# Softmax weights turned by VectorE and ScalarE, and the head norm behind the next pair's softmax

## The reference

```python
scores = einsum('bqhmd,bkhmd->bhmqk', q_blk, k) * scale      # m: the two halves of a head
scores = where(causal, scores, NEG_BIG)
probs = softmax(scores, axis=-1)
weights = probs[:, :, 0] - lam * probs[:, :, 1]
o = einsum('bhqk,bkhe->bqhe', weights, v)                    # then: RMS norm of o over the head,
branch = concatenate([o_normed, cross_out]) * silu(gate)     # and the gate
y = branch @ w_out[i]
```

## Time and profile before

| | |
|---|---|
| median of 3 runs | 956.64 us (955.88 to 961.71) |
| the profiled execution, its own time | 955.9 us |
| its span, first to last instruction | 954.1 us |
| TensorE busy | 943.2 us (99%), granted clock 0.997 |
| VectorE busy | 630.6 us (66%) |
| ScalarE busy | 474.9 us (50%) |

### The profile page before, as it was taken

How to read it: one execution, slowest core, us unless ns; L and a number is a source line. 1 busy time by engine, 2 the same in 40 slices (tenths; PEclk the granted TensorE clock), 3 DMA queues, 4 the chain that set the end, 5 groups by cost and what they waited for, 6 DMA issues and landing times.

```text
span 954.1 us, 14081 instructions
## 1 busy us (share of the span) xinstructions
PE 943.2 (99%) x5148; PEld 810.9 (85%) x5148; DVE 630.6 (66%) x868; ACT 474.9 (50%) x726; POOL 1.2 (0%) x9
## 2 busy tenths in 40 slices
PE   8999999999999999999999999999999999999996
PEld 7888888888888888888888888888888888888885
DVE  5877665666666666655595546457878778886555
ACT  6767544444444443344465355345465465464541
POOL 0000000000000000000000000000000000000000
PEclk9999999999999999999999999999999999999998
DMA  9757466666666665665576646565655755746562
GB/s 337 235 168 261 153 186 197 200 191 190 191 185 194 184 191 189 208 192 190 181 230 191 196 133 208 168 201 167 202 175 160 219 167 165 218 136 212 188 192 91
DMA packets 148778, 182.31 MB, mean 191 GB/s; under 512 B 8128, under 2 KB 116992, under 8 KB 147968
## 3 DMA queue, kind: packets, MB, share of 16 engines
q1 hardware_dynamic: 147792, 177.25, 59.8%
q10 hardware_dynamic: 944, 4.49, 1.2%
HBM read 176.48 MB, written 2.10 MB: 187 GB/s over the span
## 4 chain that ended last, share of the span: by engine, by line
PE 98%; DVE 1%; DMA 0%; ACT 0%; issue 0%; DVEq 0%; SPq 0%; ACTq 0%
PE psum L370 40%; PE psum L371 20%; PE psum L431 10%; PE psum L433 10%; PE psum L432 10%; PE psum L382 1%; PE psum L450 1%; PE psum L607 1%; PE psum L475 1%; PE psum L458 1%; PE psum L383 1%; DMA raw_ring<-in_w_kv_mem_dram 0%; PE psum L579 0%; PE psum L467 0%; PE psum L590 0%; PE psum L589 0%
## 5 line engine op out<-in xcount | busy, mean ns | idle before, releaser
L370 PE MATMUL psum<-hT_split,hi_ring 128*128 128x512 f32 x1600 | 559.3, 395 | 0.0
L923 DVE TENSOR_TENSOR lo_ring<-raw_ring,hi_ring 128x1024 fp32r<-128x1024 f32 x318 | 384.9, 1223 | 247.0 <-ACT hi_ring L656 245.5
L656 ACT ACTIVATE hi_ring<-raw_ring 128x1024 fp32r<-128x1024 f32 x318 | 335.3, 1062 | 392.8 <-PE psum L371 257.4
L371 PE MATMUL psum<-hT_split,lo_ring 128*128 128x256 f32 x1600 | 444.2, 278 | 0.0
L370 PEld LDWEIGHTS psum<-hT_split,hi_ring 128*128 128x128 f32 x1600 | 300.0, 188 | 70.5 <-issue 2.0
L371 PEld LDWEIGHTS psum<-hT_split,lo_ring 128*128 128x128 f32 x1600 | 300.7, 188 | 0.1
L431 PE MATMUL psum<-hi_ring,branchT_split 128*128 128x512 f32 x256 | 99.9, 390 | 0.0
L433 PE MATMUL psum<-hi_ring,branchT_split 128*128 128x512 f32 x256 | 99.6, 389 | 0.0
L432 PE MATMUL psum<-lo_ring,branchT_split 128*128 128x512 f32 x256 | 99.6, 389 | 0.0
L433 PEld LDWEIGHTS psum<-hi_ring,branchT_split 128*128 128x128 f32 x256 | 48.0, 188 | 10.0
L431 PEld LDWEIGHTS psum<-hi_ring,branchT_split 128*128 128x128 f32 x256 | 48.1, 188 | 10.0
(11 more groups left out here) (185 smaller groups left out, 675.7 us busy)
## 6 DMA issues: line engine op xcount, KB each, us to landing
raw_ring<-in_w_in_dram SPq DMA_DIRECT2D x224, 512.0 KB, 4.5
raw_ring<-in_w_out_dram SPq DMA_DIRECT2D x64, 512.0 KB, 4.8
raw_ring<-in_w_kv_mem_dram SPq DMA_DIRECT2D x30, 512.0 KB, 4.8
layer_area<-layer_area SPq DMA_DIRECT2D x48, 64.0 KB, 3.2
...
```

The source lines that it names most:

```text
L370: mm(o, hi[:, k, P * c:P * (c + 1)], X[:, kt, :], start=kt == 0, stop=False)
L371: last = mm(o[:, SEQ:], lo[:, k, P * c:P * (c + 1)], X[:, kt, 0:SEQ], start=False, stop=kt == KT - 1)
L656: run(whi[:, slot, :], raw[:, slot, :], ACT.Copy).then_inc(hi_ready, 1)
L923: V_.tensor_tensor(wlo[:, slot, :], raw[:, slot, :], whi[:, slot, :].bitcast(f32), SUB)\
```

## The change

`diff_turn` is gone from TensorE. VectorE turns the weights as 32x32 blocks in one instruction behind `softmax_weights` (`V_.transpose`, into the half of `prob` that is no longer needed). ScalarE then moves the blocks to their places: 16 copies of 32 partitions by 192 elements (`move_weights`), eight ahead of the key group's unit 1 and eight ahead of unit 2, in place of the one copy out of PSUM. The values (`diff_values`, `take_values`) move from key group 3 to gate group 1. `out_norm` of pair p-2 moves to VectorE's query group 3, behind the weights of pair p-1; `diff_out_turn` of p-2 to key group 3; `out_take` of p-2 to gate group 1. So the output side runs one pair later. Two sets of `o_eps` keep the sums of two pairs apart.

At the end, the output side of pair 4 and all of pair 5 behind its weights slide into the first output group. The order in which this group takes its units is changed (`OUT1_ORDER`), with the columns of pair 4 and 5 last. VectorE's loop over pairs now covers pairs 2 to 5, where it covered 1 to 4.

```diff
@@ -28,7 +28,8 @@
 XGATE_COL = GATE_COL + TOK_WIDTH
-OUT_ORDER = [0, 2, 4, 6, 8, 12, 14, 10]
+OUT0_ORDER = [0, 2, 4, 6, 8, 12, 14, 10]
+OUT1_ORDER = [0, 2, 4, 6, 12, 14, 8, 10]
 STORES = [(0, 0, 1024), (0, 1024, 2048)] + [(1, ACOLS * g, ACOLS * (g + 1)) for g in range(4)]
...
@@ -135,6 +136,8 @@
     probT = L1[:, 4608:5376].rearrange("p (h k) -> p h k", h=2)
+    prob_blocks = prob[:, :, 1, :]
+    QUADRANTS = [(a, b) for a in range(4) for b in range(4)]
     o_sb = l1(5376).rearrange("p (g e) -> p g e", g=4)
...
@@ -321,7 +324,7 @@
         for g in range(4):
-            row_group(U_OUT1 + A_UNITS * g, w_out[1], ACOLS * g, OUT_ORDER)
+            row_group(U_OUT1 + A_UNITS * g, w_out[1], ACOLS * g, OUT1_ORDER)
         for n, (t, lo_col, hi_col) in enumerate(STORES):
...
@@ -571,17 +574,8 @@
                 cross_values(1)
-        def diff_turn(p):
-
-            pe.wait_ge(w_ready, p + 1)
-            for h in range(2):
-                for b in range(3):
-                    last = nc.tensor.transpose(ps[:, 4 + h, P * b:P * (b + 1)],
-                                               prob[:, h, 0, P * b:P * (b + 1)], ident)
-            last.then_inc(wt_done, 1)
-
         def diff_values(p):
-            pe.wait_ge(wt_ready, p + 1)
+            pe.wait_ge(wt_ready, p * 16 + 16)
             for h in range(2):
...
@@ -590,8 +584,10 @@
             last.then_inc(pv_done, 1)
-        def diff_out_turn(p):
+        def diff_out_turn(p, exps=None):
             pe.wait_ge(on_ready, p + 1)
+            if exps is not None:
+                pe.wait_ge(exp_done, exps)
             for g in range(4):
...
@@ -610,10 +606,15 @@
             G, u = p * 3 + G_PAIR, p * (3 * B_UNITS) + U_PAIR
-            column_group(G, u, s, XA, at={} if first else {1: lambda: diff_scores(p - 1, second)})
-            column_group(G + 1, u + B_UNITS, 1 - s, XA,
-                         at={} if first else {2: lambda: diff_turn(p - 1), 3: lambda: diff_values(p - 1)})
-            column_group(G + 2, u + 2 * B_UNITS, s, XA, at={} if first else {2: lambda: diff_out_turn(p - 1)})
+            in_query, in_keys, in_gate = {}, {}, {}
+            if not first:
+                in_query[1] = lambda: diff_scores(p - 1, second)
+                in_gate[1] = lambda: diff_values(p - 1)
+            if not first and not second:
+                in_keys[3] = lambda: diff_out_turn(p - 2, p * 8)
+            column_group(G, u, s, XA, at=in_query)
+            column_group(G + 1, u + B_UNITS, 1 - s, XA, at=in_keys)
+            column_group(G + 2, u + 2 * B_UNITS, s, XA, at=in_gate)
         pair(0, G_PAIR % 2, first=True)
...
@@ -621,17 +622,18 @@
             pair(p + 1, (G_PAIR + 1) % 2)
-        column_group(G_XG1, U_XG1, G_XG1 % 2, XA, at={1: lambda: diff_scores(PAIRS - 1)})
+        column_group(G_XG1, U_XG1, G_XG1 % 2, XA,
+                     at={1: lambda: diff_scores(PAIRS - 1)})
         column_group(G_XG1 + 1, U_XG1 + B_UNITS, (G_XG1 + 1) % 2, XA,
-                     at={2: lambda: diff_turn(PAIRS - 1), 3: lambda: diff_values(PAIRS - 1)})
+                     at={3: lambda: diff_out_turn(PAIRS - 2, PAIRS * 8)})
         done0 = PAIRS + 1
...
                 y_wait(4 + g - 2)
-            row_group(G_OUT1 + g, U_OUT1 + A_UNITS * g, (G_OUT1 + g) % 2, XC, OUT_ORDER,
-                      before=branch_wait({0: done0 + PAIRS - 1, 5: done0 + PAIRS, 6: done0 + PAIRS + 1,
-                                          7: done0 + PAIRS + 2}),
-                      at={4: lambda: diff_out_turn(PAIRS - 1)} if g == 0 else {},
+            row_group(G_OUT1 + g, U_OUT1 + A_UNITS * g, (G_OUT1 + g) % 2, XC, OUT1_ORDER,
+                      before=branch_wait({0: done0 + PAIRS - 2, 4: done0 + PAIRS - 1, 5: done0 + PAIRS,
+                                          6: done0 + PAIRS + 1, 7: done0 + PAIRS + 2}),
+                      at={1: lambda: diff_values(PAIRS - 1), 5: lambda: diff_out_turn(PAIRS - 1)} if g == 0 else {},
                       half_first=g == 3)
...
@@ -867,9 +869,12 @@
                 cross_take(1)
-        def take_weights(p):
-            act.wait_ge(wt_done, p + 1)
-            run(probT, ps[:, 4:6, 0:3 * P], ACT.Copy).then_inc(wt_ready, 1)
+        def move_weights(p, first, last):
+            act.wait_ge(blocks_turned, p + 1)
+            for a, b in QUADRANTS[first:last]:
+                to = probT.rearrange("p h (k a r) -> p h k a r", k=3, a=4)[32 * b:32 * b + 32, :, :, a, :]
+                block = prob_blocks.rearrange("p h (k b r) -> p h k b r", k=3, b=4)[32 * a:32 * a + 32, :, :, b, :]
+                run(to, block, ACT.Copy).then_inc(wt_ready, 1)
         def take_values(p):
...
@@ -892,8 +897,8 @@
             column_group(G + 1, u + B_UNITS, 1 - s,
-                         at={} if first else {2: lambda: take_weights(p - 1), 3: lambda: take_values(p - 1)})
-            column_group(G + 2, u + 2 * B_UNITS, s)
+                         at={} if first else {1: lambda: move_weights(p - 1, 0, 8), 2: lambda: move_weights(p - 1, 8, 16)})
+            column_group(G + 2, u + 2 * B_UNITS, s, at={} if first else {1: lambda: take_values(p - 1)})
             tanh_of(G + 2, val1, tanh1)
...
@@ -904,10 +909,11 @@
         column_group(G_XG1 + 1, U_XG1 + B_UNITS, (G_XG1 + 1) % 2,
-                     at={2: lambda: take_weights(PAIRS - 1), 3: lambda: take_values(PAIRS - 1)})
+                     at={1: lambda: move_weights(PAIRS - 1, 0, 8), 2: lambda: move_weights(PAIRS - 1, 8, 16)})
         tanh_of(G_XG1 + 1, val1, tanh1)
         for g in range(4):
-            out_group(4 + g, U_OUT1 + A_UNITS * g, (G_OUT1 + g) % 2, at={1: begin_roots} if g == 1 else {})
+            out_group(4 + g, U_OUT1 + A_UNITS * g, (G_OUT1 + g) % 2,
+                      at={1: begin_roots} if g == 1 else {1: lambda: take_values(PAIRS - 1)} if g == 0 else {})
     @block.vector
...
@@ -1238,6 +1244,7 @@
         V_.tensor_copy(crossT1, cross_o).then_inc(xo_taken, 1)
+        V_.memset(cols[:, 100:101], 0.0).then_inc(o_taken, 1)
         cos2 = cosT.unsqueeze(1).broadcast_to([P, 2, SEQ])
...
@@ -1255,10 +1262,10 @@
             V_.tensor_tensor(t, t, rot, ADD).then_inc(rope_done, 1)
-        def out_norm(st, p):
+        def out_norm(st, p, parity):
             dve.wait_ge(o_copied, p * 5 + 5)
-            rsqrt(st, o_rstd, ss[:, 4:8], HEAD_DIM, o_eps)
+            rsqrt(st, o_rstd, ss[:, 4:8], HEAD_DIM, o_eps[parity])
             st.need()
...
@@ -1297,8 +1304,10 @@
             last.then_inc(w_ready, 1)
-
-        def pair(st, p, s, parity, first=False):
+            dve.wait_ge(w_ready, p + 1)
+            V_.transpose(prob_blocks, prob[:, :, 0, :]).then_inc(blocks_turned, 1)
+
+        def pair(st, p, s, parity, first=False, second=False):
             G, c, u = p * 3 + G_PAIR, p * 3 + columns_before(G_PAIR, 9), p * (3 * B_UNITS) + U_PAIR
...
@@ -1306,27 +1315,28 @@
                 rope(st, krot_loaded, p * 64 + 64, kT, krot)
-            in_query, in_keys, in_gate = {}, {}, {0: rope_queries, 3: rope_keys}
+            in_query, in_gate = {}, {0: rope_queries, 3: rope_keys}
             if not first:
                 in_query[1] = lambda: softmax_max(st, p - 1)
-                in_query[2] = lambda: softmax_weights(st, p - 1)
-                in_keys[3] = lambda: out_norm(st, p - 1)
-                in_gate[2] = lambda: out_take(st, p - 1, 1 - parity)
+                in_query[2] = lambda: softmax_weights(st, p - 1, 1 - parity)
+            if not first and not second:
+                in_query[3] = lambda: out_norm(st, p - 2, parity)
+                in_gate[1] = lambda: out_take(st, p - 2, parity)
             column_group(G, c, u, s, two(qT), at=in_query)
-            column_group(G + 1, c + 1, u + B_UNITS, 1 - s, two(kT), at=in_keys)
+            column_group(G + 1, c + 1, u + B_UNITS, 1 - s, two(kT))
             column_group(G + 2, c + 2, u + 2 * B_UNITS, s, val1, at=in_gate)
...
         pair(st, 0, G_PAIR % 2, 0, first=True)
+        pair(st, 1, (G_PAIR + 1) % 2, 1, second=True)
         before_pairs, TWO_PAIR_STEPS = st.base + st.n, 2 * (4 + 12 + 1 + 8)
-        with dve.Fori(1, PAIRS - 1, 2) as p:
-            st = Steps(dve, dve_step, before_pairs + (p - 1) * (TWO_PAIR_STEPS // 2))
-            pair(st, p, (G_PAIR + 1) % 2, 1)
-            pair(st, p + 1, G_PAIR % 2, 0)
+        with dve.Fori(2, PAIRS, 2) as p:
+            st = Steps(dve, dve_step, before_pairs + (p - 2) * (TWO_PAIR_STEPS // 2))
+            pair(st, p, G_PAIR % 2, 0)
+            pair(st, p + 1, (G_PAIR + 1) % 2, 1)
             assert st.n == TWO_PAIR_STEPS, st.n
         st = Steps(dve, dve_step, before_pairs + (PAIRS - 2) * (TWO_PAIR_STEPS // 2))
-        pair(st, PAIRS - 1, (G_PAIR + 1) % 2, 1)
         def cross_branch(i, tanhs):
...
@@ -1337,14 +1347,15 @@
         column_group(G_XG1, columns, U_XG1, G_XG1 % 2, val1,
-                     at={1: lambda: softmax_max(st, PAIRS - 1), 2: lambda: softmax_weights(st, PAIRS - 1)})
```

(8 more changed lines are left out.)

16 lines of the change are left out of this document (8 added, 8 removed).

## The result

The changed kernel takes 960.7 us, median of 20 runs (958.68 to 966.34), the kernel before on the same chips 957.24, median of 20 (955.84 to 964.15). The ratio is 1.0034, 95% interval 1.0019 to 1.0049: 0.34% slower, some 3.3 us. That is within 1% and within the range, but it is a loss clear of the interval, and not the near standstill that was forecast. The profiled execution took 961.55 us against 955.9, 5.65 more; the runs of either kernel lie in clusters a few us apart, and one execution need not sit where the median does, so I use it for places and the ratio for the amount.

What follows compares the result with a forecast made beforehand. TensorE, busy 943.2 of 954.1 us, bounds the kernel. Terms -4.0 + 0.8 + 2.3 + 0.7 = -0.2 us on 955.9 give 955.7; the median, 0.7 above that execution, makes it 956.5 us, range 952.5 to 961.

Steps and rivals of the forecast that it cites:

- The turns' price: On TensorE, six weight turns with the restart cost 0.66 us a pair; removing them from six pairs gives 4.0 us.
- Rival 4: On TensorE, the turns really cost their 273 ns each, so 9.8 us go: 947; chance 0.03.
- The block turn: On VectorE in each pair, one turn of 768 elements per partition: 0.96 us, 1.0 with its wait; bounds 0.6 and 1.8.
- Rival 2: On VectorE, the block turn takes 1.8 us; TensorE waits longer in four pairs and at the end: 960.5; chance 0.17.
- The waits in the pairs: In pairs 2 to 5, TensorE waits 0.2 us each for key unit 3's `lo`: 0.8 us lost.
- The walk: VectorE's queue in a pair, from the first weight instruction to key unit 3's `lo` done: 8.2 us.
- rival 1: VectorE has a microsecond or more in hand, TensorE never waits, all 4.0 us stay: 952.7; chance 0.20.
- The first wait at the end: TensorE waits 2.3 us ahead of the first output unit, whose `lo` stands behind the turn and pair 4's norm.
- the last paragraph on the end: First output group: ScalarE's late conversions put pair 5's norm at 874.3; TensorE waits 0.6 us, and 0.1 for the restart.
- sixteen moves (3.5): On ScalarE, copies of 192 elements at 0.22 us each, 3.5 us for sixteen; bounds 0.16 and 0.37 each.
- Rival 3: ScalarE's moves exceed 0.63 us each in the pairs; at 0.75 TensorE waits 1.9 in six: +12, 968; chance 0.05.
- the cover that I had named for the pairs: In pairs, ScalarE makes conversions a group (8.3 us) ahead of use, hiding a batch of eight moves (1.8 to 3.0).

Runs made afterwards that it cites:

- e1: Kernel before, without TensorE's six weight turns a pair; ScalarE copies the weights unturned, in the old place: 953.38 us, ratio 0.9959 to the kernel before.
- e7: Changed kernel with each block turn made twice on VectorE, the first into a free region: 966.41 us, ratio 1.0099 to the kernel before.
- e9: Changed kernel's order, but weights turned by TensorE and copied by ScalarE as before, no block turn or moves: 957.82 us, ratio 1.0020 to the kernel before.
- e3: Changed kernel with the last pair's sixteen moves ahead of ScalarE's cross-gate tanh: 958.54 us, ratio 1.0018 to the kernel before.
- e4: Changed kernel with the edits of e2 and e3, one conversion ahead of the moves, the others behind the tanh: 954.99 us, ratio 0.9983 to the kernel before.
- e8: e4 with VectorE's last norm ahead of pair 4's take, the last output turn in its own PSUM bank: 953.43 us, ratio 0.9959 to the kernel before.
- e2: Changed kernel with VectorE's first cross gate one unit later, behind the output group's first `lo`: 959.75 us, ratio 1.0034 to the kernel before.
- e5: Changed kernel with 24 identity turns on TensorE ahead of the last output turn, into an unread bank: 960.61 us, ratio 1.0036 to the kernel before.

## Why the prediction was right or wrong

The forecast was 956.5, no change; the kernel lost 3.3 us by the ratio, so the sign of the small difference was missed, though the amount is within the range. Part of that nearness is luck: the 0.8 us of waits that the forecast put into the pairs never came, and hid as much of what it missed at the end. The forecast also said that nothing under 1% can be told from none; with 20 runs of each the interval is 0.15% to either side, and the loss of 0.34% is clear. By its own steps, on the profiled execution:

| step | forecast | after |
|---|---|---|
| start | 0 | +1.1, variation |
| five periods: turns gone | -3.3 | -2.9 |
| five periods: `lo` late in four | +0.8 | 0 |
| an output turn that leaves the periods for the end | -0.35, +0.35 | as forecast |
| end: one turn gone | -0.7 | -0.7 |
| end: wait ahead of the first output unit | +2.3 | +2.7 |
| end: wait for the moves | 0 | +0.7 |
| end: wait for the last norm | +0.6 | +2.2 |
| end: unit at the lower clock | 0 | +1.6 |
| end: restarts behind these, from the distances of the output units | +0.1 | +0.7 |
| sum | -0.2 | +5.4 |

The measured sum agrees with the span, 5.5 longer, up to rounding.

- **The turns' price: right in kind.** 0.57 a period, forecast 0.66. The shortfall has a place: in the changed kernel some units without an insert take 2.83 instead of 2.77 at a granted clock of 1.00. Rival 4, that they cost 273 ns each, fell with e1.
- **The block turn: right.** 0.96 taken, 0.98 measured. By the Trainium skill (Vector Engine (DVE) Microarchitecture Reference, 3.8 The reshape front-end and per-opcode configuration) the turn sustains one element per cycle per lane; the trace agrees, its 768 elements taking less than the 1.22 of a 1024-element `lo` in about the ratio of the sizes. Rival 2 fell: the turn isn't slow. That a slow turn would be paid for in each of four pairs and again at the end is real, as e7 shows.
- **The waits in the pairs: wrong, +0.8 against 0.** The walk was right (8.2 against 8.17). Its start was not: 13.01 to 13.22 behind the first unit against 13.13 to 13.61 in the old order. This belongs to the order: counted from the scores, the softmax starts at 10.1 to 10.35 both in after and in e9, which has the new order with the turns on TensorE, and at 10.3 to 10.75 before. That it is the norm and the take, now out of VectorE's way, is argued and not shown. What rival 1 says of the waits held in the pairs, but not its condition: 0.15 to 0.35 us in hand, not a microsecond.
- **The first wait at the end: right**, 2.3 against 2.7, in its place and for its reason. Counted from the last scores, TensorE came at 21.6 (forecast 21.5) and the `lo` was done at 24.2 (forecast 23.8). Most of the difference is the gap of 0.46 ahead of L999, which no row before has and whose cause isn't shown.
- **The failed step is the last paragraph on the end**, "sixteen moves (3.5)". The term was mis-sized: a move was put at 0.22, between 0.16 and 0.37, and takes 0.38, past the upper bound. The lower anchor was misread: what starts 0.16 behind a square in the earlier trace rows is not another square but an `ACTIVATION_READ_ACCUMULATOR`. Sixteen take 6.1, 2.6 more. The times must be counted from the last scores, since these come at 832.8 in after and at 834.9 in the rows that the forecast started from. So counted the tanh came as forecast (19.3 us, forecast 19.2), but ScalarE was through with moves and conversions at 30.0, forecast 27.1. The values came to wait for the moves, and VectorE's `lo` waited 2.94 for a conversion behind them. The last norm was done at 42.7, forecast 39.4, with TensorE there at 40.6, forecast 38.9: 2.2 instead of 0.6. e3, which takes the moves out of the way and nothing else, removes both waits; e4 and e8, which also move VectorE's work, get the time back.
- **A term was missing:** the lower clock behind a long wait, 1.6. Nothing in the forecast priced a wait at more than its length. In all five profiled kernels with a wait of 2.2 us or more at the end (after, e2, e3, e5, e7), the clock fell behind one of these waits, and only one; in e4, e8 and e9, whose longest there is 1.7, it did not.
- **Rival 3**, ScalarE as the bound, asked for over 0.63 a move in the pairs. At 0.38 no wait for moves stands there; it held only in the last group, where the cover that I had named for the pairs is missing.

Left open: what sets the pace of 2.83 against 2.77, why the new order costs 0.1 to 0.2 us a period while the turns are on TensorE, and what decides whether the clock falls behind a long wait. Only the last was touched, by e5, whose one profiled execution doesn't decide it.
